# The norm of the attention output applied to the product with w_o, group by group, in one encoder layer on one core

## What is computed

```
o = concat(rms_norm(oa, out_norm_a), rms_norm(ob, out_norm_b))   # oa, ob: 512 columns each
x = x + einsum('bse,ed->bsd', o, w_o)
h2 = rms_norm(x, norm_ffn)
logits = einsum('nd,de->ne', h2, w_router)
aff = softmax(logits)
gates, idx = top_k(aff.T, 64)                                     # per expert and set
```

## Time and profile before

| what | value |
|---|---|
| median of 3 runs | 1241.86 us (1241.02 to 1241.93) |
| profiled execution | 1240.62 us |
| span of the profile | 1238.8 us |
| granted TensorE clock, mean | 0.945 |
| routing phase in it | about 497 to 641 us |

### The profile page before, as it was taken

How to read it: one execution, slowest core, us unless ns; L and a number is a source line. 1 busy time by engine, 2 the same in 40 slices (tenths; PEclk the granted TensorE clock), 3 DMA queues, 4 the chain that set the end, 5 groups by cost and what they waited for, 6 DMA issues and landing times. The chain is left out here.

```text
span 1238.8 us, 16803 instructions
## 1 busy us (share of the span) xinstructions
PE 1094.8 (88%) x5699; PEld 913.9 (74%) x5699; DVE 920.0 (74%) x1236; ACT 767.5 (62%) x1005; POOL 270.9 (22%) x272
## 2 busy tenths in 40 slices
PE   5995899879758899599953999999999999999996
PEld 4874678768547787488842788888888888888885
DVE  4567999815678897133576788988888888898883
ACT  5433788723348887233242777777777877777772
POOL 1244001103455521022123011101111111110211
PEclk9996999989979999799975999999999999999999
DMA  7000000020010000566216899999999999999992
GB/s 266 18 1 1 1 1 35 19 85 1 1 69 35 35 35 18 206 209 222 97 56 212 330 361 393 393 395 395 395 395 395 394 394 410 394 395 396 395 360 34
DMA packets 70109, 255.40 MB, mean 206 GB/s; under 512 B 5736, under 2 KB 7867, under 8 KB 70059
## 3 DMA queue, kind: packets, MB, share of 16 engines
q1 hardware_dynamic: 62730, 229.07, 47.6%
q0 software_dynamic: 7328, 25.68, 7.3%
HBM read 233.76 MB, written 20.97 MB: 206 GB/s over the span
## 5 line engine op out<-in xcount | busy, mean ns | idle before, releaser
L1570 DVE TENSOR_TENSOR lo<-raw,hi 128x2048 fp32r<-128x2048 f32 x189 | 427.8, 2290 | 63.8 <-ACT hi L1505 43.5
L1505 ACT ACTIVATE hi<-raw 128x2048 fp32r<-128x2048 f32 x192 | 364.5, 1918 | 72.3 <-PE ps L1422 65.7
L1420 PE MATMUL ps<-hi,xehi 128*128 128x512 f32 x512 | 202.0, 395 | 3.2 <-DVE xelo L1575 3.2
L1422 PE MATMUL ps<-hi,xelo 128*128 128x512 f32 x512 | 200.7, 392 | 0.0
L1421 PE MATMUL ps<-lo,xehi 128*128 128x512 f32 x512 | 200.7, 392 | 0.0
L1420 PEld LDWEIGHTS ps<-hi,xehi 128*128 128x128 f32 x512 | 97.1, 190 | 23.6 <-issue 2.9
L1422 PEld LDWEIGHTS ps<-hi,xelo 128*128 128x128 f32 x512 | 96.9, 189 | 20.2
L1421 PEld LDWEIGHTS ps<-lo,xehi 128*128 128x128 f32 x512 | 97.0, 189 | 19.7
L938 ACT ACTIVATE prob<-ps,nmax 128x512 f32<-128x512 f32 x128 | 87.9, 687 | 23.8 <-DVE nmax L993 21.6
L849 PE MATMUL ps<-ident,prob 128*128 128x128 f32 x512 | 79.7, 280 | 20.2 <-DVE probTlo L989 19.9
L849 PEld LDWEIGHTS ps<-ident,prob 128*128 128x128 f32 x512 | 61.4, 143 | 46.9 <-issue 22.8
(11 more groups left out here) (213 smaller groups left out, 2047.2 us busy)
## 6 DMA issues: line engine op xcount, KB each, us to landing
raw<-in_w_gate SPq DMA_DIRECT2D x64, 1024.0 KB, 7.3
raw<-in_w_up SPq DMA_DIRECT2D x64, 1024.0 KB, 7.3
raw<-in_w_down SPq DMA_DIRECT2D x64, 1024.0 KB, 7.7
w_raw<-in_w_in SPq DMA_DIRECT2D x8, 592.0 KB, 12.3
x<-in_x SPq DMA_DIRECT2D x8, 512.0 KB, 4.1
woraw<-in_w_o SPq DMA_DIRECT2D x4, 1024.0 KB, 4.9
o<-attention_out SPq DMA_DIRECT2D x8, 512.0 KB, 3.8
xr<-in_x SPq DMA_DIRECT2D x8, 512.0 KB, 4.7
```

The source lines that it names most:

```text
L1420: pe.matmul(ps[:, dst[n], :], xehi[:, c, :], hi[w][:, cols], start=c == 0, stop=False)
L1422: last = pe.matmul(ps[:, dst[n], :], xelo[:, c, :], hi[w][:, cols], start=False, stop=c == KD - 1)
L1505: act.activation(hi[s][:], raw[s][:], ACT.Copy).then_inc(hi_done, 1)
L1570: dve.tensor_tensor(lo[s][:], raw[s][:], hi[s][:].bitcast(F32), ALU.subtract).then_inc(lo_done, 1)
```

## The change

The rows of `o` are no longer scaled before the transposes. `othi` and `otlo` are made from the rows as they are, and w_o's product is kept apart by group: chunks 0 to 3 (group 0) go to PSUM banks 2 and 3, chunks 4 to 7 (group 1) to banks 4 and 5. DVE multiplies each sum with that group's factor per row and adds: first xr + ro0 * WO[0], in place in xr, then that + ro1 * WO[1] to x1. It can do the first while PE works on group 1.

The banks for this come from h2's transposes, which have one bank now (6) and go in two fours with a wait for ACT's copy between them, and from `LG` and `AT`, which share bank 7. The accesses to that bank are put in sequence: PE transposes aff of block t-3 before the router product of block t-2, and the latter waits for `at_done`, the affT copy; DVE makes that copy ahead of the maximum, no longer behind aff.

```diff
-    OT, WO, HT, LG, AT = (0, 1), banks(2, 2), (4, 5), ps[:, 6, 0:EXPERTS], ps[0:EXPERTS, 7, 0:P]
+    OT, WO, HT, LG, AT = (0, 1), (banks(2, 2), banks(4, 2)), 6, ps[:, 7, 0:EXPERTS], ps[0:EXPERTS, 7, P:2 * P]
...
             @block.tensor
             def _(pe):
-                def h2_transposes(u):
+                def h2_transposes(u, b):
                     pe.wait_ge(h2_done, u + 1)
-                    if u:
-                        pe.wait_ge(ht_copied, 2 * u)
...
+                    if u or b:
+                        pe.wait_ge(ht_copied, 2 * u + b)
...
                         if u:
-                            pe.wait_ge(x1_done, 2 * u)
+                            pe.wait_ge(group_added, 2 * u)
                         for c in range(KD):
-                            if c == KD // 2 and t >= 2:
-                                h2_transposes(t - 2)
+                            if c in (KD // 2, KD // 2 + 2) and t >= 2:
+                                h2_transposes(t - 2, (c - KD // 2) // 2)
+                            group = WO[c // (C_K // P)]
+                            if u and c == C_K // P:
+                                pe.wait_ge(x1_done, 2 * u)
...
                     if t < T:
-                        pe.wait_ge(on_done, 2 * t + 2)
+                        pe.wait_ge(o_loaded[t % 3], 16 * (t // 3 + 1))
...
+                    if t >= 3:
+                        u = t - 3
+                        pe.wait_ge(aff_done, u + 1)
+                        pe.transpose(AT, aff, k["ident"][:]).then_inc(at_ready, 1)
                     if 2 <= t <= T + 1:
                         u = t - 2
...
                         if u == 0:
                             pe.wait_ge(small_loaded, 32)
                         else:
-                            pe.wait_ge(lexp_done, u)
+                            pe.wait_ge(at_done, u)
...
-                    if t >= 3:
-                        u = t - 3
-                        pe.wait_ge(aff_done, u + 1)
-                        if u:
-                            pe.wait_ge(at_done, u)
-                        pe.transpose(AT, aff, k["ident"][:]).then_inc(at_ready, 1)
...
             @block.vector
...
-                        dve.wait_ge(wo_done, u + 1)
+                        dve.wait_ge(wo_done, 2 * u + 1)
+                        dve.wait_ge(ro_done, u + 1)
...
-                            dve.tensor_tensor(x1[u % 2][:, cols], WO[:, cols], xr[u % 3][:, cols], ALU.add).then_inc(x1_done, 1)
+                            dve.scalar_tensor_tensor(out=xr[u % 3][:, cols], in0=WO[0][:, cols], scalar=ro(u)[:, 0:1],
+                                                     in1=xr[u % 3][:, cols], op0=ALU.mult, op1=ALU.add).then_inc(group_added, 1)
+                        dve.wait_ge(wo_done, 2 * u + 2)
+                        for n in range(2):
+                            cols = slice(n * BANK, (n + 1) * BANK)
+                            dve.wait_ge(group_added, 2 * u + n + 1)
+                            dve.scalar_tensor_tensor(out=x1[u % 2][:, cols], in0=WO[1][:, cols], scalar=ro(u)[:, 1:2],
+                                                     in1=xr[u % 3][:, cols], op0=ALU.mult, op1=ALU.add).then_inc(x1_done, 1)
...
-                    if t + 1 < T:
-                        group_rows(t + 1)
...
+                    if t >= 3:
+                        u = t - 3
+                        dve.wait_ge(at_ready, u + 1)
+                        dve.tensor_copy(k["affT"][:, u * P:(u + 1) * P], AT).then_inc(at_done, 1)
                     if 2 <= t <= T + 1:
                         u = t - 2
                         dve.wait_ge(lg_ready, u + 1)
...
-                        dve.wait_ge(at_ready, u + 1)
-                        dve.tensor_copy(k["affT"][:, u * P:(u + 1) * P], AT).then_inc(at_done, 1)
```

More of the change, by code:

```diff
@@ L1127, in _ @@
             def _(pe):
-                def h2_transposes(u):
+                def h2_transposes(u, b):
                     pe.wait_ge(h2_done, u + 1)
-                    if u:
-                        pe.wait_ge(ht_copied, 2 * u)
[L1132 to L1136, removed]
+                    if u or b:
+                        pe.wait_ge(ht_copied, 2 * u + b)
+                    for i in range(4):
+                        c = 4 * b + i
+                        last = pe.transpose(ps[:, HT, i * P:(i + 1) * P], h2[u % 2][:, c * P:(c + 1) * P], k["ident"][:])
+                    last.then_inc(ht_ready, 1)
                 for t in range(T + 3):
@@ L1149, in _ @@
                                     cols = slice(n * BANK, (n + 1) * BANK)
[L1150 to L1153, removed]
+                                    last = pe.matmul(group[:, cols], lhs[:, c, :], wo[rhs][:, c, cols],
+                                                     start=(c % (C_K // P) == 0 and rhs == "hi" and lhs is othi[u % 2]),
+                                                     stop=(c % (C_K // P) == C_K // P - 1 and lhs is otlo[u % 2]))
+                            if c % (C_K // P) == C_K // P - 1:
+                                last.then_inc(wo_done, 1)
                     if t < T:
-                        pe.wait_ge(on_done, 2 * t + 2)
+                        pe.wait_ge(o_loaded[t % 3], 16 * (t // 3 + 1))
                         if t:
@@ L1165, in _ @@
                         if t > T:
-                            h2_transposes(u)
+                            for b in range(2):
+                                h2_transposes(u, b)
                         if u == 0:
@@ L1203, in _ @@
                                 act.wait_ge(lg_ready, u)
-                            act.activation(h2T[:, 4 * b:4 * b + 4, :], ps[:, HT[b], :].rearrange("p (a c) -> p a c", a=4),
+                            act.activation(h2T[:, 4 * b:4 * b + 4, :], ps[:, HT, :].rearrange("p (a c) -> p a c", a=4),
                                            ACT.Copy).then_inc(ht_copied, 1)
@@ L1209, in _ @@
                             if t >= 2 and b == 0:
-                                act.wait_ge(wo_done, t - 1)
+                                act.wait_ge(wo_done, 2 * (t - 1))
                             act.activation(othi[t % 2][:, 4 * b:4 * b + 4, :], ps[:, OT[b], :].rearrange("p (a c) -> p a c", a=4),
@@ L1227, in _ @@
                 steps = Steps(dve, vsteps)
[L1228 to L1235, removed]
                 for t in range(T + 3):
```

5 lines of the change are left out of this document (3 added, 2 removed).

## The result

| what | before | after |
|---|---|---|
| median | 1241.56 us (4 runs, 1241.02 to 1241.93) | 1291.03 us (4 runs, 1285.54 to 1293.32) |
| profiled execution | 1240.62 us | 1290.55 us |
| span | 1238.8 us | 1288.8 us |
| granted TensorE clock, mean | 0.945 | 0.923 |

The changed kernel is slower: ratio 1.039, interval 1.037 to 1.041. That is 49.5 us; forecast were 46 (1288, range 1269 to 1299).

A forecast was written before the change was run, and what follows sets the result against it. PE's own work was taken to bound the routing turns (14.72 us). Terms 22.5 + 16.0 + 7.6 + 0.3 = 46.4 us on 1240.6 gave 1287.0, forecast as a median of 1288, range 1269 to 1299.

The forecast's parts named there:

- stalls, turns 3 to 7: Router product waits for the affT copy behind h2: 4.5 us in each of five turns, 22.5 us.
- clock behind them: Lower PE clock after each stall: router product +1.7, w_o's product +1.5; 3.2 each, 16.0 us for five.
- tail: After the last turns, the final router product waits for block 6's affT copy behind two top-eight rounds: 7.6 us.
- turns without a stall: Longer group 1 adds make otlo up to 0.1 us later in two or three turns: 0.3 us.
- head: Routing start: transposes no longer await scaled rows, but the second block's squares cover it; gain 0, otherwise up to 3.4 us.
- POOL: POOL's steps before h2 get shorter without DVE's row scaling beside them: 0.2 us taken off each stall.
- A: Rival: the clock holds through PE's gaps in the turns; 1269 to 1272 us, chance 0.17.
- B: Rival: the clock stays down longer, w_o's product starting from the bottom; 1.7 + 3.4 per stall, 1298 us, chance 0.15.
- C: Rival: the previous turn's affT copy meets the wait, no stalls, only the head gains; 1238.5 us, chance 0.03.
- D: Rival: the change does nothing, head covered and waits met; 1242 us, chance 0.03.
- The edits at nothing: In the steady turn, dropping row scaling and splitting h2's transposes cost 0; four adds instead of two cost 0 to 0.3.

The follow-up runs named there:

- the kernel with the filled gap: Changed kernel plus 18 unread 512-column matmuls ahead of the router product's wait in turns 3 to 8: 1268.35 us, ratio 1.023.
- the kernel with the order alone: Kernel before, with only the affT transpose ahead of the router product, its wait on at_done, and the affT copy ahead of the maximum: 1289.77 us, ratio 1.040.
- the mended change: Changed kernel with affT transpose in mid product, squares of block 1 behind the first othi copy, block 6's affT copy ahead of top-eight rounds: 1238.66 us.
- the kernel with the gap of 1.90: Changed kernel with DVE's affT copy right behind otlo and ahead of h2, instead of behind h2: 1268.7 us, ratio 1.023.
- the kernel with the gap filled: Changed kernel with the affT copy behind otlo, plus 8 unread 512-column matmuls in PE's gap: 1256.12 us, ratio 1.013.

## Why the prediction was right

The code and the mechanism were right, and the terms can be set side by side. Measured are differences of the two profiled executions, whose spans lie 50.0 apart.

| term | forecast | measured | from |
|---|---|---|---|
| stalls, turns 3 to 7 | 5 x 4.5 = 22.5 | 5 x 4.49 = 22.4 | router product at E+5.36 against E+0.87 |
| clock behind them | 5 x 3.2 = 16.0 | 5 x 3.6 = 18.1 | 114.07 - 73.54 - 22.4 |
| tail | 7.6 | 7.4 | 20.34 - 12.93 |
| turns without a stall | 0.3 | 0.4 | 13.20, 14.83, 14.86 against 13.08, 14.69, 14.73 |
| head | 0 | -0.1 | first product 15.00 against 15.14 behind the attention phase |
| sum | 46.4 | 48.2 | |

Stall and clock are 8.1 a turn together, forecast were 7.7. Where the line between them runs depends on the measure: the start of the router product gives 4.49 and 3.6; the kernel with the filled gap 4.4 and 3.7; PE's idle time and its longer work 4.2 and 3.9. The forecast's 4.5 has 0.1 taken off for the transpose of aff, so it is to be held against 4.4; by the weight loads, in which it was reckoned, the product came 4.60 later (E+5.59), where E+5.6 and 4.6 were forecast.

The remaining 1.8 of the 50.0 lie ahead of the routing phase (its start moved from 496.55 to 498.46), where the kernels are the same; the profiles of the experiments have that point anywhere from 495.7 to 498.5. So it is put down to the scatter of the executions and not to the change.

*The wait.* Its length came from one row, the start of h2's neighbour in the earlier trace rows, its place and its count of seven from the printed order of the two engines. The gap was 4.22, forecast "about 4.3"; not under 4, so h2 was rightly placed. The tail came out step by step: its first router product ended at 8.97 behind block 7's product (forecast 8.9), its last copy at 20.34 (20.6). That moving transpose and copy alone, with or without the rest of the change, takes the loss away or makes it, was shown both ways (1289.77 and 1246.52).

*POOL.* The 0.2 us taken off for it are there: a gap of 4.22 with the row scaling gone, 4.40 where it is still there, and 4.20 in that same kernel's turn 7, which scales nothing; POOL's last step (L1105) takes 0.56 without it, its shortest in the earlier trace rows, and 0.67 to 0.68 beside it in the kernel with the order alone. By the Trainium skill, page "SBUF — State Buffer", section "Who interferes with whom", a tensor_scalar in its two-port mode locks GpSimd out of the port pair they share; the trace agrees, with these 0.2 us.

*The clock* is the mis-sized term: 3.2 forecast, 3.6 measured (up to 3.9 by the other measures), 2 us or more over all. The router product cost 1.6 on the mean, forecast 1.7 (in turn 3 it took 2.94, since the clock fell only within it). The step that failed was the next: "here 3.6 us of router product have already gone by, so I take 1.5" for w_o's product. The granted clock stayed at 0.50 until 569.3, 593.1, 613.6, 637.6 and 661.4 in the five turns, that is for 4.6, 5.5, 2.5, 4.4 and 5.4 us of w_o's product: 4.5 on the mean, which costs 2.3. So it stayed down as long as at the head (4.4), and the router product in front took nothing off.
The clock's total was measured by itself, with the unread matmuls: 22.7 us with the tail's share in it. Of that the profiles show 18.4 in the turns and 1.6 in the tail; the rest is of the size by which runs differ.
By the Trainium skill, page "TensorE: Matmul & The Clock Gate", section "HAM oscillation", the fall is paid anew in each turn; the trace agrees, five times of five. The gaps that the page warns of are longer than some that did it here, though, and there the measurement decides (below).

*The rivals.* A (clock held, 1269 to 1272) is what the filled gap gives, 1268.35: its price was right and its condition wrong. Its ground, the gap of 1.70 that did no harm, was weaker than the prediction took it for: a gap of 1.90, in the place in question, lowered the clock in all five turns. B's price, 5.1 a stall, came up in no turn in full: the largest, turn 4, has 23.43 - 14.71 - 4.49 = 4.2. C and D fell with the row of waits.

*The edits at nothing.* The row scaling, the split of h2's transposes and the four adds cost 0.4 us together in the three turns without a stall (table); that they do no more in the others is shown, to within the scatter of the runs, by the kernel that has none of them and is as slow. At the head the cover was as named: the squares of the second block. ACT stands 4.28 us for its transfer, and othi comes behind them. "Up to 3.4" was its worth in the prediction; with the squares moved, the unscaled rows gave 3.8.

## What to carry to other kernels

Before two small results share a PSUM bank, find the instruction that will free it and look where it stands in its engine's program in *this* turn: a count that is met "by the copy of the block before" can still be the last thing that engine does. Moving such a step to an earlier place costs a few tenths a turn, while the wait on an in-order TensorE queue costs the stall and the clock on top, here nearly as much again. When a change frees an engine that was not the bound, look for what stands in front of the freed step; here one edit of ACT's order gave 2.7 us (1238.68 against 1241.38), as much as the same edit together with the mended change.

## What was not expected of the hardware

Short gaps lowered the clock in this loop: 1.90 us in five turns of five (12.6 us in all), 0.97 us in three of five, and 0.76 us once. Yet a gap of 1.83 us in turn 1 of the changed kernel left it up, as the one of 1.70 had done before:

```profile
529.52 0.73 PE L1152 MATMUL ps<-wohi,othi 128*128 128x512 f32 x2 [1.83 <-DVE otlo L1253]
```

Behind that gap comes w_o's product, of 512 columns; behind the others the router product, of 16 columns. Whether the narrow product or the moment of the gap makes the difference stays open: no run put a wide product behind the gap of turns 3 to 7. Without any gap the same router product left the clock at 1.00 in every turn.

Nor is the fall the same each time: the gaps of the changed kernel's turns are 4.22 to 4.24 us, its turns 22.01 to 23.43. What differs is when the clock falls and how long it stays down. Read in stretches of 0.1 us, it fell 5.0 us after PE's last matmul in turn 3, within the router product, and 2.1 us after it in turn 6, in the middle of the gap; it stayed low for 6.8, 10.2, 6.8, 10.2 and 10.2 us. In the kernel with the gap of 1.90 it fell in turn 3 at 561.4, 3 us after the gap had ended (558.31), when w_o's product was running. So what stands just ahead of a fall in the trace need not be its cause; there the kernel with the gap filled showed the cause.
